# Expert rows gated when they are copied and summed by adding transfers, and the first input rows issued ahead of the constants: a streaming MLA, GLA and mixture-of-experts layer on one core

## The reference

```
h  = rmsnorm(x)
cq, ckv, kpe, gq, gk, gv, glr, gr, ga, gb = split(h @ w_in)
x += (sigmoid(ga) * (MLA(...) @ w_branch_a) + sigmoid(gb) * (GLA(...) @ w_branch_b)) @ w_out
h2 = rmsnorm(x)
# two of 32 experts for each token, chosen in one of 4 groups, with gates g1, g2
x += g1 * expert_e1(h2) + g2 * expert_e2(h2)
y  = rmsnorm(x)
expert_e(h) = (silu(h @ w_gate[e]) * (h @ w_up[e])) @ w_down[e]      # 1024 -> 512 -> 1024
```

## Time and profile before

| | us |
|---|---|
| median of 3 runs | 1165.0 |
| lowest, highest | 1163.5, 1165.24 |
| the profiled execution | 1161.22 |
| its span in the trace | 1159.4 |
| PE busy in it | 1033.1 |
| DVE, ACT, POOL busy | 371.2, 277.0, 235.1 |

### The profile page before, as it was taken

One profiled execution on the slowest core, in us unless ns is written; L12 is line 12 of the kernel. 1 busy time (PEld: TensorE's weight loads), 2 busy tenths in 40 slices (PEclk: granted clock), 3 DMA queues, 4 the chain that ended last, 5 costly groups with the idle time before them and its releaser, 6 DMA issues. The chain is left out here.

```text
span 1159.4 us, 15302 instructions
## 1 busy us (share of the span) xinstructions
PE 1033.1 (89%) x6359; PEld 716.0 (62%) x6359; DVE 371.2 (32%) x704; ACT 277.0 (24%) x443; POOL 235.1 (20%) x131
## 2 busy tenths in 40 slices
PE   3999999999989997999999899988788887778896
PEld 2996778777978887999999633333333333333332
DVE  6038332333367419241222612211111111110117
ACT  5325433445344524222210400000000000000003
POOL 3331211212321226443331011111110111100100
PEclk9999999997999979999999899989999888898899
DMA  8343331111211122334346799999999999999994
GB/s 203 76 84 91 110 100 38 40 52 37 76 45 28 46 64 67 97 110 133 92 167 279 266 384 426 425 426 426 428 426 427 428 429 425 429 425 427 424 412 165
DMA packets 109519, 267.57 MB, mean 231 GB/s; under 512 B 22525, under 2 KB 89373, under 8 KB 96242
## 3 DMA queue, kind: packets, MB, share of 16 engines
q1 hardware_dynamic: 104754, 258.06, 58.3%
q0 software_dynamic: 4704, 8.64, 2.0%
HBM read 256.12 MB, written 18.17 MB: 237 GB/s over the span
## 5 line engine op out<-in xcount | busy, mean ns | idle before, releaser
L1389 PE MATMUL proj<-we,xsT 128*64 128x512 f32 x512 | 250.7, 647 | 67.8 <-DMA we<-in_w_exp_up 61.5
L1391 PE MATMUL proj<-we,xsT 128*64 128x512 f32 x512 | 251.2, 648 | 0.0
L879 POOL TENSOR_TENSOR wlo<-raw,whi 128x1024 fp32r<-128x1024 f32 x70 | 162.4, 2320 | 410.1 <-PE proj L1017 397.5
L1389 PEld LDWEIGHTS proj<-we,xsT 128*64 128x64 f32 x512 | 73.3, 149 | 211.6 <-issue 196.8
L1017 PE MATMUL proj<-hT_hi,whi 128*128 128x272 f32 x704 | 150.2, 295 | 10.7 <-DVE hT_lo L269 8.2
L1017 PE MATMUL proj<-hT_hi,wlo 128*128 128x272 f32 x704 | 148.1, 292 | 0.0
L1017 PE MATMUL proj<-hT_lo,whi 128*128 128x272 f32 x704 | 147.8, 292 | 0.0
L2284 DVE TENSOR_TENSOR hg<-hg,proj 64x512 f32<-64x512 f32 x32 | 22.1, 690 | 310.2 <-ACT hg L1842 295.7
L1017 PEld LDWEIGHTS proj<-hT_hi,whi 128*128 128x128 f32 x704 | 111.9, 191 | 15.0 <-DVE hT_lo L269 8.3
L1547 ACT CAST whi<-raw 128x1024 fp32r<-128x1024 f32 x70 | 69.7, 999 | 214.2 <-PE proj L1017 208.3
L1842 ACT ACTIVATE hg<-proj 64x512 f32<-64x512 f32 x30 | 17.7, 590 | 424.7 <-PE proj L1391 424.7
(11 more groups left out here) (328 smaller groups left out, 1422.3 us busy)
## 6 DMA issues: line engine op xcount, KB each, us to landing
we<-in_w_exp_gate SPq DMA_DIRECT2D x31, 2048.0 KB, 32.1
we<-in_w_exp_up SPq DMA_DIRECT2D x31, 2048.0 KB, 36.5
we<-in_w_exp_down SPq DMA_DIRECT2D x31, 2048.0 KB, 38.9
raw<-in_w_in SPq DMA_DIRECT2D x43, 512.0 KB, 3.8
x_rows<-in_x_prompt SPq DMA_DIRECT2D x8, 512.0 KB, 4.7
raw<-in_w_branch_b SPq DMA_DIRECT2D x8, 512.0 KB, 3.9
raw<-in_w_out SPq DMA_DIRECT2D x8, 512.0 KB, 3.9
zc<-expert_out SPq DMA_DIRECT2D x4, 1024.0 KB, 17.4
```

The lines of the kernel that those rows point to most:

```text
L879: nc.gpsimd.tensor_tensor(lo[:, 0:c], raw[n % NRAW][:, 0:c], hi[:, 0:c].bitcast(F32), ALU.subtract).then_inc(w_split, 1)
L1389: pe.matmul(proj[0:SLOTS, s, 0, :], xsT[:, k, cols], wg[:, k * FF:(k + 1) * FF], start=(k == 0), stop=(k == KD - 1))
L1391: mm = pe.matmul(proj[64:64 + SLOTS, s, 0, :], xsT[:, k, cols], wu[:, k * FF:(k + 1) * FF], start=(k == 0), stop=(k == KD - 1))
```

## The change

In the head, SP issues the identity (the first 128 columns of `cst`, 64 KB) after input tile 0, all gain columns as one transfer after tile 1, and the rest of the constants (581 KB) after the first three weight tiles. ACT starts with a square root on a scratch column, after two memsets. ACT takes the high part of weight tile 0 before the root of tile 3, and the high parts of weight tiles 1 and 2 after those of all input tiles. POOL splits weight tile 0 first and takes the low parts of tiles 0, 1 and 2; DVE takes those of 3 and 4 after its other work. PE does 3 extra matmuls of 512 columns at the start, one after each turned tile and two after the last (`warm`, nothing reads them). The first product is written out: its two terms with the high part of the input for half of the tokens after three tiles, for the other half after five, and the third term at the end.

In the router, `last_gates` and its ten PE transposes go. DVE makes two one-hot products with the gates (128 x 240 each), PE turns them with 40 small matmuls into `slot_gate`, a gate for each slot of each block, and DVE copies it. `pick` is a plain comparison.

With the experts, the copy of the result to `yo` multiplies with the slot's gate, on DVE and (last two) on ACT. So `expert_out` holds gated rows. ACT does a square root on a scratch column before the last copies.

In the tail, SP's loads of `zc` go. POOL issues five transfers that add the first choice from `expert_out` to the rows of `X` in SBUF, waits for all of them, and issues five for the second choice. All `add_gated` and `second_rows` go; `add_last` waits for all ten transfers.

```diff
@@ sync: order of the first loads
         for i in range(NT):
             sp.dma_start(X[0:ROWS[i], i, :], x_src(i)).then_inc(rows_loaded[i], 16)
             if i == 0:
-                sp.dma_start(cst[:, :], t["shape_constants"]).then_inc(const_loaded, 16)
-                sp.dma_start(g_mix[:, :], t["g_mix_cols"]).then_inc(const_loaded, 16)
...
+                sp.dma_start(cst[:, 0:n], t["shape_constants"][:, 0:n]).then_inc(first_loaded, 16)
+            if i == 1:
+                sp.dma_start(gains[:, :], t["gain_columns"]).then_inc(first_loaded, 16)
+        for w in range(NRAW):
+            load_weights(w)
+        sp.dma_start(cst[:, n:], t["shape_constants"][:, n:]).then_inc(const_loaded, 16)
@@ tensor: the first product
+        pe.wait_ge(consts_set, 1)
+        warm(WARM_ROWS)
+        pe.wait_ge(first_loaded, 32)
...
+            warm(WARM_HALVES if i == NT - 1 else 1)
+        pe.wait_ge(w_split, 1)
+        for half in range(2):
+            pe.wait_ge(hT_hi_ready, (3, NT)[half])
+            for n, (w, r) in enumerate(order[0:2]):
...
         pe.wait_ge(hT_ready, NT)
-        product("cq", 0)
+        w, r = order[2]
@@ scalar: order of roots and high parts
-        act.wait_ge(consts_set, 1)
+        act.wait_ge(root_set, 1)
+        nc.scalar.activation(st_x[:, 1, :], st_x[:, 1, :], ACT.Sqrt)
         for i in range(3):
             x_root(i)
-        for i in range(NT):
+        high(0)
+        x_root(3)
+        hT_high(nc, act, 0, hTf_ready, hT_hi, hT_f, hT_hi_ready)
+        x_root(4)
+        for i in range(1, NT):
             hT_high(nc, act, i, hTf_ready, hT_hi, hT_f, hT_hi_ready)
-            if i + 3 < NT:
-                x_root(i + 3)
-            if 1 <= i <= NHIGH:
-                high(i - 1)
+        for n in range(1, NHIGH):
+            high(n)
@@ vector: gates by slot, and the copy of an expert's result
-        run(v.tensor_tensor(both_gates, O[:, :, :, NE - 2:NE], ...))
-        v.tensor_tensor(last_gates[:, :, :], both_gates[:, 0], both_gates[:, 1], ALU.add)...
+        for c in range(2):
+            last = v.tensor_tensor(token_at[:, c], is_blk[:, c], gate[:, c, :]..., ALU.mult)
+        last.then_inc(slot_gates_ready, 1)
...
-            v.tensor_copy(yo[:, s, :], proj[:, s, 1, :])
+            v.tensor_scalar(yo[:, s, :], proj[:, s, 1, :], slot_gate[:, cols], None, ALU.mult)
@@ gpsimd: the sums
+        pool.wait_ge(x2_copied, NT)
+        pair_rows = ys.rearrange("(t x) d -> t (x d)", x=4)
+        for c in range(2):
+            if c:
+                pool.wait_ge(added[0], 16 * NT)
+            for i in range(NT):
+                pool.dma_start(X[0:ROWS[i], i, :], pair_rows[i * P:i * P + ROWS[i], c * D:(c + 1) * D], accum_op=ALU.add)\
+                    .then_inc(added[c], 16)
@@ vector: the tail
         def add_last(i):
             r = ROWS[i]
+            dve.wait_ge(added[1], 16 * NT)
             dve.wait_ge(picked, i + 1)
...
         for i in range(NT):
             add_last(i)
-            if i + 2 < NT:
-                add_gated(i + 2, 0)
...
             if i:
                 root_inverse(i - 1)
-            if i > 1:
-                final(i - 2)
+                final(i - 1)
```

More of the change, by code:

```diff
@@ L78 @@
 NCONST = _c
+GAINS = []
+for _name, _n in (("g_norm_mix", KD), ("g_qnorm", 2), ("g_kvnorm", 1), ("g_gla_norm", 2), ("g_norm_ffn", KD), ("rows", KD)):
+    GAINS.append((_name, sum(g[2] for g in GAINS), _n))
+NGAIN = sum(g[2] for g in GAINS)
 def shape_constants():
@@ L313, in _build @@
     shift_b = R("shift_b", [1, NE], BF16)
[L314 to L319, removed]
+    gains = R("gains", [P, NGAIN])
+    g_mix, g_q, g_kv, g_gla, g_ffn, g_rows = (gains[:, at:at + n] for _, at, n in GAINS)
     G_FIN = R.at
@@ L592, in _build @@
     second_done = sem("second_done")
+    slot_gates_ready = sem("slot_gates_ready")
+    slot_gates_done = sem("slot_gates_done")
+    slot_gates_copied = sem("slot_gates_copied")
+    added = [sem(f"added{c}") for c in range(2)]
     onehots_ready = sem("onehots_ready")
@@ L1022, in product_part, with warm @@
                 mm.then_inc(proj_done, 1)
-        pe.wait_ge(const_loaded, 112)
+        def warm(n):
+            for _ in range(n):
+                pe.matmul(proj[:, 1, 0, :], ones[:, :], S_smp[:, 0:2, :].rearrange("p a b -> p (a b)"), start=True, stop=True)
+        pe.wait_ge(consts_set, 1)
+        warm(WARM_ROWS)
+        pe.wait_ge(first_loaded, 32)
         for i in range(NT):
@@ L1034, in _ @@
             mm.then_inc(xT_ready, 1)
-        pe.wait_ge(hT_ready, NT)
-        product("cq", 0)
+            warm(WARM_HALVES if i == NT - 1 else 1)
+        taken = take("cq", 0)
+        order = ((whi[0], hT_hi), (wlo[0], hT_hi), (whi[0], hT_lo))
+        pe.wait_ge(w_split, 1)
+        for half in range(2):
+            pe.wait_ge(hT_hi_ready, (3, NT)[half])
+            for n, (w, r) in enumerate(order[0:2]):
+                for k in range(KD):
+                    pe.matmul(proj[:, taken[1], half, 0:HALF], w[:, k * P:(k + 1) * P], r[:, k, half * HALF:(half + 1) * HALF],
+                              start=(n == k == 0), stop=False)
+        pe.wait_ge(hT_ready, NT)
+        w, r = order[2]
+        for half in range(2):
+            for k in range(KD):
+                mm = pe.matmul(proj[:, taken[1], half, 0:HALF], w[:, k * P:(k + 1) * P], r[:, k, half * HALF:(half + 1) * HALF],
+                               start=False, stop=(k == KD - 1))
+        mm.then_inc(proj_done, 1)
+        pe.wait_ge(const_loaded, 16)
         product("cq", 1)
@@ L1484, in last_rows @@
                 mm.then_inc(picked, 1)
-        def second_rows(i, start):
-            out = pick_out(i)
-            if i == 1:
-                pe.wait_ge(turns_ready, 1)
-            pe.wait_ge(rows_loaded[i], 48)
-            for half in range(2):
-                pe.matmul(out[:, half, :], second[:, i - 1, :], zc[i][:, 1, half * FF:(half + 1) * FF], start=start, stop=False)
         def up_half(k):
```

113 lines of the change are left out of this document (40 added, 73 removed).

## The result

The changed kernel takes 1167.7 us (median of 12 runs, 1165.5 to 1169.0); the kernel before took 1164.0 us beside it (12 runs, 1162.3 to 1165.7). The ratio is 1.003, with a 95% interval of 1.0021 to 1.0039: 3.7 us slower, just outside the 0.2% that the prediction called no change. Forecast was 1158.

What follows compares the result with a forecast made beforehand. Bound: PE idle in the head, PE full in the middle, transfers at their limit in the experts. Span 1159.4 - 9 + 0.5 + 1.6 = 1152.5, its time 1154.3; with 3.8 to the median, 1158; range 1154 to 1170.

Steps and rivals of the forecast that it cites:

- T: Tail: the time when all sums have landed, put at 1145.7; the end at T + 15.3, 1161.0.
- the plain price: Tail: an adding transfer takes what a plain one of its size takes; the tail then costs 1.6 us more.
- Two reads for each sum: Rival, tail: sums need two reads and are slower; tail 12.2 us more, in all +3.7, 1169 us; chance 0.28.
- a wait for all of them waits for the last: Tail: some of the 16 transfer engines end earlier than others; share only 0.38 from 1138 to 1140.
- The head: Head: first product ends at 26.8 instead of 35.8, 9 us less, bounds 6 and 11.
- So DVE's subtraction ends with POOL's: Head: DVE's two low parts take 4.5 us beside POOL's; all low parts by 22.5 to 24.6.
- The router: Router: first turned rows wait 0.4 to 0.5 us for the new gates; 0.5 us more, bounds 0 and 1.
- The rest of the tail: Tail after T: sums and scalings 11.8 us, a gap of 1.5, store 2.4; end at T + 15.3.
- up to 4 us: Tail: down weights landing this much later give picks of tile 0 by 1141, tile 3 by 1145.5; PE not the bound.

Runs made afterwards that it cites:

- plain_pool: Changed kernel with POOL's ten adding transfers made plain copies into another buffer, both choices left out of the sums: 1156.8 us, ratio 0.9934.
- tile_waits: Changed kernel, but a tile's second addition waits only for its first and its sum for its own two: 1155.6 us, ratio 0.9937.
- head_only: Kernel before with only the new head (loads, roots, extra matmuls, split product); router, copies and tail as before: 1157.6 us, ratio 0.9944.
- lows_apart: Changed kernel with plain-load tail; DVE takes low parts of tiles 2 to 4, POOL splits weight 1 after all low parts: 1154.1 us, ratio 0.9922.
- head_whole: As head_only, but PE waits for all low parts, then runs the first product whole: 1162.9 us, ratio 0.9995.
- dve_waits: Changed kernel, but DVE's sum of a tile waits only for its own two additions; POOL still waits for all five: 1160.6 us, ratio 0.9971.
- pool_waits: Changed kernel, but POOL's second addition of a tile waits only for its first; sums still wait for all ten: 1163.3 us, ratio 0.9994.

## Why the prediction was wrong

**The step that failed is one term: T.** "T = 1145.7, if an adding transfer takes what a plain one of its size takes", 25.7 us after the last scatter's landing. It is 36.2. The choice in it, "I take the plain price", was wrong: with plain copies in the same order and with the same waits T is +25.8. That this meets the forecast so closely is partly luck. In `plain_pool` the first five had landed at +16.4, where 17.6 was forecast, and the second five took 9.4 us more, where 8.1 was forecast. The doubled packet was measured by itself (0.34 against 0.165 us). The rival "Two reads for each sum", a chance of 0.28, had T at +36.3, the first five landed at +22.9 (POOL went on at +21.8) and the kernel at 1169 us (1167.7). The Trainium skill (page "Collectives: The Full Stack", section "The bandwidth ceiling: the fold count and why AG ≠ RS ≠ AR") puts the adding steps of a collective at half the copies' rate, and these rows agree. That two source reads are the reason, as it says, no run here shows.

My reason for the plain price was that the second read is from SBUF, beside one from HBM. The traces don't say which part of a packet is doubled. They say that it is.

**The prediction did not say that the tail's order was its own cost.** It had the wait for all five in its sum ("a wait for all of them waits for the last") and counted 1.5 us for issue and first bytes. It didn't ask what the tail would be without the waits, nor where the loss could be got back. Both waits together are worth 12.1 us, more than the doubled price, and the change is a gain once they are gone, though only by its head (`tile_waits` 0.9937, `head_only` 0.9944). The rows for it were there in the kernel before: the share of 0.38 from 1138 to 1140.

**The head: mechanism right, size off by 2.5 us.** Forecast 9, with bounds of 6 and 11; measured 6.5. The table loads left tile 0's path as put. Weight tile 0 was cast at 12.20 instead of 10.4, so POOL's low parts ran until 23.6 instead of 21. "So DVE's subtraction ends with POOL's" missed that POOL has weight 1's split next: DVE was still beside it at 27.2. The forecast was 22.5 to 24.6, and `lows_apart` got 23.5 by taking that split out of the way. The high terms started at 21.09 (forecast about 20), and their going first is the gain, as said; `head_whole` shows it. One price in this step was misread: an extra matmul of 512 columns takes 1 us and not 0.5, since the "four" in 1.98 us are the records of two matmuls (the two extra ones after the last tile are four records in 1.98 us too). Also, the 7.45 us for 48 matmuls, from which the 5 and 2.5 us were taken, were partly at the lower clock (0.66 us a pair until 31.2); the last 16 took 2.25.

**The router: the step was longer, and it didn't count.** The turned rows are 1.8 us later against the gather, not 0.5. Of that, 1.1 us are the 40 matmuls, which took 2.88 us at the lower clock, not 1.77. Between the gather and the last scatter nothing of it is left. In that stretch the transfers are full (share 1.00 from 660 to 1100), which hid the delay. I had let it through to the end.

**The rest of the tail was right.** The end is T + 15.8. The forecast wrote T + 15.3, but its own three terms (11.8, 1.5 and 2.4) add up to 15.7. The down weights landed later (a median of 30.7 against 25.6 us, "up to 4 us" forecast, 5.1 measured) and were not the bound.

**The account.** The forecast for the span was -6.9 us, and it is +4.2. T makes 10.5 of the 11.1 between them, the end after T 0.5 and the head 2.5; against them stand 0.5 us of the router that weren't lost and 1.9 us more gained between head and tail (1.4 to the first gather, the rest among the experts). These 1.9 are within what the same instructions scatter by between profiles here (621.2 and 623.8 us from the head's cast to the first gather in `dve_waits` and `pool_waits`; 621.2 in the changed kernel, 622.6 before), and I don't explain them.

## What to carry to other kernels

- A transfer that adds saves an engine's pass but was paid in transfer time, at twice a copy's. Use it where the transfer engines have room, and price it before it goes where they are the bound.
- When a batch of transfers waits for a whole batch, look at the transfer share just before the wait ends. Here a remainder that was the work of some two of sixteen engines held up the rest, and one semaphore for each tile was worth 12 us of the tail, three times the 3.7 us that the change had lost.
- Where an operation is a sum of terms with different sources, start the terms whose sources come first: the split of one product carried nearly the whole gain of the head, part of it because TensorE stayed at work and kept its clock.

## What the runs showed of the hardware

- Adding packets from DRAM into SBUF took the transfer engines 0.34 us where plain ones from the same queue took 0.165 (0.315 and 0.164 over a whole batch), and moved 179 GB/s at a full share. POOL needed 4.5 us to issue five of them, 2.7 us for five plain ones.
- The sixteen transfer engines didn't finish a batch together: share 0.48 for 4 us, then 0.13 for 3.4 us, before the five transfers had landed.
- DVE and POOL slowed each other in subtractions of two SBUF operands: two on DVE took 5.86 us beside POOL, three took 3.25 with POOL idle for most of them; POOL's split of a weight tile took 3.34 us beside DVE and 2.40 alone (`lows_apart`).
- TensorE's clock after a wait without work: after 5.50 us idle a pair of matmuls took 0.66 us (`head_whole`), with the high terms ahead of it 0.41; 40 small matmuls took 2.88 us at a granted clock of 0.50 and 1.77 at 1.00.
- The granted clock on record can read 1.00 where the rows are at the lower level: the first 30 us of the kernel before, with pairs of 0.66 us.
